# Third stage of a two-block model: projections in f32r on split halves, modulation pieces spread out, their rows turned on VectorE

## The reference

```
x = LN(a*x + even_mixer(x))        # gated delta rule and windowed attention
x = LN(a*x + conv_ffn(x))
x = LN(a*x + odd_mixer(x))         # the third stage: this change
x = LN(a*x + conv_ffn(x))
for i in 0, 1:                     # second block
    shift, scale, gate = split(silu(c) @ ada_w[i, 0] + ada_b[i, 0])   # modulation
    x = LN(a*x + (1 + gate) * mixer(x*(1 + scale) + shift))
    ... the same once more with a mixture of experts in place of the mixer
```

```
q_c, k_c, v_c, q_d, k_d, v_d, r_d, g_d = split(x @ w_in)
lam = exp(sum(lp0*lp1)) - exp(sum(lp2*lp3)) + lam0
o_c = (softmax(q1 k1' + bias) - lam * softmax(q2 k2' + bias)) v_c    # 4 heads, causal
o_c = rms_norm(o_c) * (1 - lam0)
o_d = gated linear attention of (q_d, k_d, v_d) with decay log_sigmoid(g_d @ w + b) / 16
o_d = rms_norm(o_d) * silu(r_d)
out = concat(o_c, o_d) @ w_out
```

## Time and profile before

| | us |
|---|---|
| median of 3 runs | 1826.91 (1821.27 to 1826.99) |
| the profiled execution: span | 1825.7 |
| PE busy | 1750.6 |
| DVE busy | 959.6 |
| ACT busy | 655.1 |
| POOL busy | 229.9 |

### The profile page before, as it was taken

How to read it: one execution, slowest core, us unless ns; L and a number is a source line. 1 busy time by engine, 2 the same in 40 slices (tenths; PEclk the granted TensorE clock), 3 DMA queues, 4 the chain that set the end, 5 groups by cost and what they waited for, 6 DMA issues and landing times. The chain is left out here.

```text
span 1825.7 us, 25869 instructions
## 1 busy us (share of the span) xinstructions
PE 1750.6 (96%) x10464; PEld 1292.0 (71%) x10464; DVE 959.6 (53%) x1782; ACT 655.1 (36%) x1102; POOL 229.9 (13%) x217
## 2 busy tenths in 40 slices
PE   9999999999999999999999989999899999899987
PEld 8788976699887555899888764434489898544433
DVE  1275643688642564788455663333267867533223
ACT  1025323466530234666446431111144455311111
POOL 0000000154211130263002402000000200010000
PEclk9899999999999899999999999999999999999999
DMA  8322286446534585455343659999934555799995
GB/s 309 146 93 92 81 299 267 171 161 223 185 139 162 184 339 214 185 208 185 120 179 139 256 197 421 420 420 419 391 128 160 187 208 207 304 419 420 420 421 228
DMA packets 51853, 443.05 MB, mean 243 GB/s; under 512 B 5900, under 2 KB 6160, under 8 KB 9104
## 3 DMA queue, kind: packets, MB, share of 16 engines
q1 hardware_dynamic: 47664, 426.79, 60.1%
q0 software_dynamic: 2480, 8.92, 1.4%
q10 hardware_dynamic: 1584, 5.61, 0.8%
HBM read 440.25 MB, written 1.05 MB: 242 GB/s over the span
## 5 line engine op out<-in xcount | busy, mean ns | idle before, releaser
L82 PE MATMUL ps<-ringx,arena 128*64 128x512 f32 x1056 | 275.7, 594 | 7.1 <-DMA ringx<-in_mg 3.1
L88 ACT ACTIVATE arena<-ps 128x384 f32<-128x384 f32 (+5 forms) x233 | 101.5, 436 | 495.6 <-PE ps L82 301.4
L82 PE MATMUL ps<-xsplit_f,wsplit_f 128*128 128x256 f32 x2112 | 256.1, 284 | 4.2 <-ACT xsplit_f L88 2.7
L82 PEld LDWEIGHTS ps<-xsplit_f,wsplit_f 128*128 128x128 f32 x2112 | 254.1, 192 | 6.6 <-ACT xsplit_f L88 4.2
L82 PE MATMUL ps<-ring,arena 128*64 128x512 f32 (+1 forms) x704 | 228.0, 597 | 7.5 <-DMA ring<-in_mu 6.1
L91 DVE TENSOR_TENSOR wsplit_f<-ring,wsplit_f 128x1024 fp32r<-128x1024 f32 x132 | 180.5, 1371 | 70.0 <-ACT wsplit_f L88 70.0
L82 PEld LDWEIGHTS ps<-ringx,arena 128*64 128x64 f32 x1056 | 90.2, 137 | 168.3 <-issue 153.9
L82 PE MATMUL ps<-xTs,ring 128*128 128x256 f32 (+1 forms) x960 | 188.8, 357 | 2.3 <-ACT xTs L88 1.8
L82 PEld LDWEIGHTS ps<-xTs,ring 128*128 128x128 f32 x960 | 163.5, 193 | 24.6 <-issue 6.4
L88 ACT ACTIVATE wsplit_f<-ring 128x1024 fp32r<-128x1024 f32 x132 | 138.2, 1051 | 57.5 <-PE ps L82 56.5
L91 DVE TENSOR_TENSOR ringlo<-ring,ringhi 128x1024 fp32r<-128x1024 f32 x88 | 120.7, 1387 | 58.1 <-ACT ringhi L88 57.9
(11 more groups left out here) (196 smaller groups left out, 2452.5 us busy)
## 6 DMA issues: line engine op xcount, KB each, us to landing
ring<-in_ada SPq DMA_DIRECT2D x24, 2048.0 KB, 7.8
ring<-in_wu SPq DMA_DIRECT2D x22, 2048.0 KB, 8.1
ringx<-in_mg SPq DMA_DIRECT2D x44, 1024.0 KB, 20.7
ringx<-in_mu SPq DMA_DIRECT2D x44, 1024.0 KB, 23.9
ringx<-in_md SPq DMA_DIRECT2D x44, 1024.0 KB, 26.1
ring<-in_md SPq DMA_DIRECT2D x24, 1024.0 KB, 25.4
ring<-in_mg SPq DMA_DIRECT2D x24, 1024.0 KB, 20.8
ring<-in_mu SPq DMA_DIRECT2D x24, 1024.0 KB, 23.9
```

Of the source, the lines that this page charges most:

```text
L82: return self.e.matmul(o, l, r, start=start, stop=stop, skip_group_check=True)
L88: return self.e.activation(o, i, f, **k)
```

## The change

- The projections of the stage other than the first four tiles and the small gate product: po4 to po15, "vc", "vd" and the down projection go through `tile_split`, `rows_split`, `rows_half` and `down_split` on split halves. That is 28 parts (`ODD_CH`): 28 high halves on ACT, 28 low halves on DVE, written over the weights in the ring. x is split too (`xth`, `O.xtl`), and the outputs (`O.ohi`, `O.olo`).
- The modulation pieces: four stand ahead of the loop, the others sit at other places in `AMONG`; `LOADS` has them between the other weights, and `BESIDE` and a rule of the oldest slot place them.
- The row block of a piece is turned on DVE: `flip32` transposes its 32x32 blocks into SBUF, in place of ACT's copy, and PE's second product has 32 columns of weights (`fold32`) and 4 columns moving, in four column groups. This holds for the pieces of the first stage as well.
- The causal mask is added to the bias table once at the end of the first stage, in place of in the third.

```
-AMONG = [("po", 12), ("ada", 0), ("po", 13), ("ada", 1), ("po", 14), ("po", 15), ("vd", 0), ("ada", 2), ("vd", 1)] \
-    + [("ada", k) for k in range(3, ADA)]
+AMONG = [("po", 12), ("ada", 4), ("po", 13), ("ada", 5), ("po", 14), ("ada", 6), ("po", 15), ("vd", 0), ("vd", 1),
+         ("ada", 7), ("ada", 8), ("ada", 9), ("ada", 10), ("ada", 11), None, ("ada", 12), None, None]
...
+ODD_CH = chunks("T", ("wo", 1), ("wo", 2)) + chunks("R", ("wov", 0)) + chunks("T", ("wo", 3)) + chunks("R", ("wov", 1)) \
+    + chunks("D", ("woo", 0), ("woo", 1))
...
-    out += [("wo", 0), ("wo", 1), ("wo", 2), ("wov", 0), ("wo", 3)] + ada[:3] + [("wov", 1)] + ada[3:]
+    out += [("wo", 0), ("wo", 1), ada[0], ("wo", 2), ada[1], ("wov", 0)] + ada[2:4] + [("wo", 3)] + ada[4:7] + [("wov", 1)]
+    out += ada[7:] + [("woo", 0), ("woo", 1)] + ffn(1)
...
+BESIDE = {("ada", 3, 0): ("ada", 2, 4), ("wov", 1): ("ada", 2, 5), ("ada", 3, 1): ("ada", 3, 0), ("ada", 3, 2): ("wo", 3),
+          ("ada", 3, 3): ("wov", 1), ("ada", 3, 4): ("ada", 3, 1), ("ada", 3, 5): ("ada", 3, 2), ("woo", 0): ("ada", 3, 3),
+          ("woo", 1): ("ada", 3, 4)}
... (ada_piece on PE)
-                t.wait_ge(*a("adr", i, j))
+                t.wait_ge(*v("adr", i, j))
                 b = bank("ada", i, j)
+                blocks = adr[(k - 1) % 2].rearrange("p (m a n) -> p a n m", m=4, a=4)
                 for c in range(4):
-                    r = mm(b[:, c:c + 1], adr[(k - 1) % 2][:, 128 * c:128 * c + 128], four, True, True)
+                    r = mm(b[32 * c:32 * c + 32, 0:4], fold32, blocks[:, c, 0, :], True, True)
... (odd on PE)
             for n in range(9, 12):
-                proj_T(("wo", 2), "po", n, n % 4, 3)
-            proj_rows(("wov", 0), "vc", 512)
+                tile_split(2, n - 4, "po", n)
+            ada_piece(1, 1)
+            rows_split(2, 8, "vc")
+            ada_piece(1, 2)
+            ada_piece(1, 3)
             for u, k in DIFF:
... (odd on DVE)
+            for i in range(9, 12):
+                low_half(2, i)
+            ada_piece(1, 1)
             for h in range(2):
                 evac_rows("vc", h, O.vc[:, h, :])
-            tt(O.TC, TP, bc(K("cm").rearrange("p (a n) -> p a n", a=1), [128, 4, 256]), ALU.add).then_inc(s_dve, v.did())
+            for i in range(12, 15):
+                low_half(2, i)
+            ada_piece(1, 2)
+            ada_piece(1, 3)
...
+                kind, j = AMONG[k] or (None, 0)
+                if kind == "po":
+                    low_half(2, j + 3)
+                elif kind == "vd" and j == 0:
+                    low_half(2, 19)
+                elif kind == "ada":
                     ada_piece(1, j)
+                if 14 <= k < 18:
+                    low_half(2, k + 6)
```

More of the change, by code:

```diff
@@ L273, in all_slots @@
         else:
-            if name in ELSEWHERE:
-                i = ELSEWHERE[name]
-            else:
-                i = turn % SLOTS
-                turn += 1
+            if name in BESIDE:
+                i = out[BESIDE[name]][0]
+            else:
+                i = min(range(SLOTS), key=lambda k: (LOADS.index(last[k]) if k in last else -1, k))
+            turn = i + 1
         used[i] = used.get(i, 0) + 1
@@ L461, in emit @@
     scb = gate[:, 0:256].rearrange("p (k n) -> p k n", k=8)
-    four = small[:, 218:219]
+    fold32 = gate[:, 256:288]
     fold16 = small[:, 380:396]
@@ L559, in emit @@
         O.oT = rows(O.oTf, 8, 256)
-        O.TC = m.take(1024).rearrange("p (h n) -> p h n", h=4)
+        O.xT = O.oT
         O.gdT = m.take(256)
@@ L572, in emit @@
         O.qd, O.kdT, O.kdt, O.Sg = (rows(m.take(256), 2, 128) for _ in range(4))
+        low_part = m.top
+        m.take(2048)
+        O.rhi = fr(st, "odd_high", 4, 1024)
+    with ExitStack() as st:
+        st.enter_context(nc.sbuf_tensor("below_odd_x", [128, low_part], F32))
+        O.xtl = fr(st, "odd_xlow", 8, 256)
+    with ExitStack() as st:
+        O.ohi, O.olo = (fr(st, f"odd_out{i}", 8, 256) for i in range(2))
     with ExitStack() as st:
@@ L779, in down_part, with x_low, rows_half @@
                 t.note("used", src)
+        def x_low(n):
+            return O.xtl if n == 2 else xtl
+        def rows_half(n, i, tag, h):
+            b, tk = bank(tag, h), slice(h * 128, h * 128 + 128)
+            for c in range(4):
+                _, hi, lo = chunk(n, i + c)
+                t.wait_ge(*v("split", n, i + c))
+                for k in range(2):
+                    for q, (w, xx) in enumerate(((hi, xth), (lo, xth), (hi, x_low(n)))):
+                        r = mm(b, xx[:, 2 * c + k, tk], w[:, k, :], c + k + q == 0, (c, k, q) == (3, 1, 2))
+                if h and c < 3:
+                    r.then_inc(s_pe, t.did())
+                    t.note("part", n, i + c)
+            r.then_inc(s_pe, t.did(tag, h))
+            if h:
+                t.note("part", n, i + 3)
+                t.note("used", CHUNKS[n][i][0])
         def tile_split(n, i, tag, j, ring=R8):
@@ L1219, in odd, with gla_sums @@
                     .then_inc(s_pe, t.did("glo", h))
-            banks = [bank(("dn", 2), i) for i in range(4)]
-            t.wait_ge(*v("dfn", 1))
-            down_part(banks, ("woo", 0), O.oT, (0, 1))
-            for n in range(2):
-                t.wait_ge(*a("gl_sq", n))
-                rms_sums(("gln", n), O.two[n])
-            t.note("early", 2)
-            down_part(banks, ("woo", 0), O.oT, (2, 3))
-            t.wait_ge(*v("gl_out", 1))
-            down([("woo", 0), ("woo", 1)], ("dn", 2), O.oT, banks)
+            def gla_sums():
+                for n in range(2):
+                    t.wait_ge(*a("gl_sq", n))
+                    rms_sums(("gln", n), O.two[n])
+                t.note("early", 2)
+            down_split(2, ("dn", 2), 20, lambda f: O.ohi[:, f, :], lambda f: O.olo[:, f, :], lambda f: v("osplit", f // 2),
+                       {2: gla_sums})
             t.note("pre", 2)
@@ L1715, in ada_piece @@
         def ada_piece(s, k):
+            if 0 <= k < 12:
+                i, j = 2 * s + k // 6, k % 6
+                v.wait_ge(*t("adr", i, j))
+                if k > 1:
+                    v.wait_ge(*t("ada", 2 * s + (k - 2) // 6, (k - 2) % 6))
+                v.own()
+                v.flip32(adr[k % 2], ps("adr", i, j)).then_inc(s_dve, v.did("free", "adr", i, j))
+                v.note("adr", i, j)
             if k <= 0:
@@ L1756, in even @@
                 if n == 6:
-                    red(four, ident[:, 0:128:32], ALU.add).then_inc(s_dve, v.did())
+                    red(fold32, ident.rearrange("p (a j) -> p j a", a=4), ALU.add).then_inc(s_dve, v.did())
                     v.wait_ge(*a("sc"))
@@ L2049, in odd @@
                 stt(o, o, C("lnw"), O.rT[:, n * 512:n * 512 + 512], ALU.mult, ALU.mult).then_inc(s_dve, v.did("gl_out", n))
+            for n in range(2, 4):
+                low_out(n)
+            for i in range(25, 28):
+                low_half(2, i)
             v.note("early", 2)
@@ L2059, in gates @@
             v.note("gdT")
+        def gates():
             v.wait_ge(*t("lga"))
@@ L2763, in odd @@
             stage_begins(1)
-            x_transposed(2, after(1))
+            x_transposed(2, after(1), (xth, O.xtl), xT=O.xT)
+            for i in range(4):
+                high_half(2, i)
             for n in (4, 5, 6, 7):
                 tile(n)
+                high_half(2, n)
+            high_half(2, 8)
             a.wait_ge(*v("la"))
@@ L2773, in odd @@
             a.note("lam")
-            for n in (10, 11):
-                tile(n)
+            high_half(2, 9)
+            tile(10)
+            high_half(2, 10)
+            tile(11)
+            for i in range(11, 15):
+                high_half(2, i)
             Bq = O.Bc.rearrange("p (n t m) -> p n t m", n=2, t=2)
```

116 lines of the change are left out of this document (74 added, 42 removed).

## The result

The changed kernel takes 1844.3 us (1841.8 to 1847.5, 4 runs), the kernel before on the same chip 1827.0 us (1821.3 to 1828.2): ratio 1.0099 with a 95% interval of 1.0083 to 1.0115. That is 17.3 us slower, where 1829.5 us and no measurable change were forecast, and it lies above the range of 1810 to 1841.

A forecast was written before the change was run, and what follows sets the result against it. PE was taken to bound the kernel before, DVE the changed loop. Third stage + 8.6 and first stage - 6.0 gave + 2.6 on the profiled 1825.7; with the runs' median 1.2 above that, 1829.5 us, range 1810 to 1841.

The forecast's parts named there:

- What PE loses in work: Third stage's tiles, row products, down projection and pieces: 28 us less PE work, and 6 in the first stage.
- First stage, - 6: First stage: twelve cheaper second products save 8.0 us, of which 2.0 run into the wait for "woe"; 6 remain.
- First stretch, + 11.2: Third stage up to the loop: PE idles 9.7 us for a turn behind halves of `wo` 3; loop begins 11.2 later.
- The splits of `wo` 1 are ready by then: Third stage's start: with ACT free from 543.5 and DVE from 542.9, splits are ready when f32 tiles end near 550.5.
- the rule that the prediction weighed and priced at 0.15 us: Low halves beside POOL's adds: the skill says POOL contends with DVE's two-input instructions; the rows gave 0.15 us more.
- Loop up to low half 16: Loop's first part: low half 16 waits for the `wov` 1 load; DVE idles 12.3 us, PE about 10.
- Loop from there, 62.9 + 8 us: Loop from low half 16 to "glo": DVE is the bound, with 62.9 us of work and 8 allowed for waits.
- Third stretch: From "glo" to the stage's end: 29.8 us, before 33.5; next stage's second turn 2.5 us later behind the end.
- A: The two waits don't both bind, or DVE's gaps in the loop are shorter: 1818.5 us, chance 0.22.
- C: DVE bounds the loop from 636 to 706, slowed by POOL, with PE clock loss behind pauses: 1841 us, chance 0.20.
- B: PE stays the bound throughout: 1793 us, up to 5 less if the clock stays up, chance 0.08.
- D: Pieces' new second product gains nothing: + 6 in the first stage, hidden in the loop; 1835, within the forecast's 0.50.

The follow-up runs named there:

- e9: e6 with DVE making each of the nine low halves 15 to 23 twice, 18 more instructions: kernel 4.8 us longer than e6.
- e13: The kernel before with only 28 idle PE products added in the third stage's loop: ratio 1.0019.
- e6: The changed kernel with `wo` 3 and `wov` 1 loaded early into other slots, pieces from 3 on made later in the loop: 1827.7 us.
- e8: e6 with 28 idle products on PE ahead of its waits in the third stage's loop: 1822.5 us.
- e1: The kernel before with only the modulation pieces' part of the change (row turned on DVE, new second product): 1820.2 us, ratio 0.9971.
- e12: e7 with the 28 idle PE products in the third stage's loop: 1824.3 us, ratio 0.9984.
- e11: e1 with the 28 idle PE products in the third stage's loop: 1816.4 us, ratio 0.9952.
- e7: e6 with the third stage's last product taken back to f32: 1822.0 us, ratio 0.9977.
- e4: The changed kernel with DVE's turns of pieces 2 and 3 ahead of low halves 12 to 14 and `wov` 1 asked for earlier: 1834.3 us.
- e5: e4 with the third stage's last product taken back to f32, without its low and high halves: 1827.8 us.
- e14: The changed kernel with the 28 idle PE products in the third stage's loop, its late loads left: 1846.6 us, ratio 1.0116.

## Why the prediction was wrong

The sum was 14.7 us short: 8.3 in the loop, 3.2 ahead of it, 2.1 behind it, and the rest in no part that can be named. The step that failed is the loop's sum over DVE alone: 62.9 us of work, which was about right, and 8 us for its waits, which took 17.3.

**What PE loses in work: right.** A tile is 24 products 0.12 us apart, the second product of a piece takes 0.22 to 0.24 (0.25 was taken, between 0.13 and 0.92), the turn 0.72 (0.69). Over all PE's busy time fell by 28.8 us of the 34 counted; some of the work ran at the lower clock. The rows, PE's in the first stage:

```profile
291.16 0.22 PE L82 MATMUL ps<-tmpn,gate 128*32 128x4 f32 x8
292.18 0.24 PE L82 MATMUL ps<-tmpn,gate 128*32 128x4 f32 x8 [0.80 <-DVE tmpn L111]
295.21 4.97 PE L82 MATMUL ps<-ring,arena 128*128 128x512 f32 x7 [2.79 <-DMA ring<-in_woe]
```

**First stage, - 6: right.** "woe" is waited for longer (2.8 us, before 1.4). The profiled executions are 9.9 us apart at the third stage's start, but of this 3.5 is the clock's (last section); two executions alike in that, e9 and e13, start it at 520.98 and 527.36: 6.4 us.

**First stretch, + 11.2: the wait right, the stretch 3.2 short.** PE idled 9.8 us where 9.7 was worked out, behind the instruction named. The stretch grew by 14.4. The 3.2 are two more waits of PE for low halves, 3.8 us where 0.5 was counted. For the first, 2.0 us at 542 and 546, the sentence that failed is "The splits of `wo` 1 are ready by then". It had DVE free from 542.9 on the clock of the execution before, which is 533.0 here; DVE was then at the splits of x and stayed there to 539. DVE, POOL and PE at that place:

```profile
533.52 5.52 DVE L91 TENSOR_TENSOR odd_xlow<-arena,xth 128x512 fp32r<-128x512 f32 x2
538.96 6.69 DVE L91 TENSOR_TENSOR ringall<-ring,odd_high 128x1024 fp32r<-128x1024 f32 x2
```
```profile
533.28 11.29 POOL L91 TENSOR_TENSOR xs<-xs,lnp 128x1024 f32<-128x1024 f32 x4 [7.08 <-ACT arena L88]
```
```profile
542.47 0.36 PE L82 MATMUL ps<-xth,odd_high 128*128 128x256 f32 x1 [1.87 <-DVE ringall L91]
...
579.44 0.50 PE L82 MATMUL ps<-odd_high,xth 128*128 128x512 f32 x1 [1.76 <-DVE ringall L91]
```

The wait of 1.76 us is the second, for low half 9, which the prediction priced at 0.5; no POOL instruction runs there. DVE takes that half only at 578.17, behind the gate's scans.

In the first wait two splits of 0.7 us each took 5.5 and two of 1.22 took 6.7, just while POOL added rows of 128x1024 at 2.8 us each (2.4 each in the kernel before, where no split stood beside them). This is the rule that the prediction weighed and priced at 0.15 us: the Trainium skill (GPSIMD Engine Reference, Specifications) lets POOL contend with VectorE's instructions of two SBUF inputs. The trace agrees, and by 2 us for each instruction, but at a place where the prediction hadn't looked.

**Loop up to low half 16: the waits right, 2.3 us short.** DVE idled 13.7 us there (12.3 worked out), PE 8.7 (about 10); the stretch took 28.5 us in place of 26.2.

**Loop from there, 62.9 + 8 us: wrong, and this is the step that decides.** From the start of low half 16 to the glo products it was 76.9 us in place of 71.0. "So the bound has changed engines", said the prediction; it expected DVE over 85% busy. DVE was busy 59.6 of 76.9 us, 78%, PE 74%. So its row was no longer than worked out, but its idle time, of which 8 us were allowed, was 17.3. Neither is the bound by itself. Units and levels go from PE to DVE, to ACT or POOL, and back; both engines take them in one fixed order, and each stands idle for a part of the other's time. On e6, e9 prices DVE's work at 0.4 to 0.6 of its length, and e8 shows that more work on PE doesn't lengthen the loop. To add up one engine's row and to put a small allowance on it gives a lower bound of such a loop, not its length. The kernel before had PE busy 91.3 and DVE 55.7 of its loop's 98.6 us; with 8.7 less on PE and 8.0 more on DVE the loop took 97.4 (e1), with 16.6 less on PE, 18.5 more on DVE and no late load 98.6 (e6).

The second part of the same step is the clock. The prediction left it to the rivals at 2 us. The tile that follows PE's first pause shows its price, in PE's timeline after:

```profile
603.20 0.58 PE L82 MATMUL ps<-xth,odd_high 128*128 128x256 f32 x1
603.58 0.41 PE L82 MATMUL ps<-odd_xlow,odd_high 128*128 128x256 f32 x1
603.79 0.41 PE L82 MATMUL ps<-xth,ringall 128*128 128x256 f32 x1
...
606.34 0.28 PE L82 MATMUL ps<-xth,odd_high 128*128 128x256 f32 x1
606.46 0.28 PE L82 MATMUL ps<-odd_xlow,odd_high 128*128 128x256 f32 x1
```

Products follow each other in 0.21 us at first and in 0.12 from 606.1: the lower and the higher of the two levels. So the tile takes 4.3 us instead of 2.86. An engine that waits more often also works more slowly. What idle products got back of this in the loop was 1.9, 1.7 and 3.6 us (e8, e12, e11), in e12 lost again in the tail.

**Third stretch: 29.8 us worked out, 32.4 measured; second turn + 2.0 (2.5).** The products themselves are right, but they start in pieces as halves and left sides come. Against the kernel before the tail loses 0.9 us instead of winning 1.2.

**The sum.** Worked out: - 6.0 + 11.2 - 1.4 - 1.2 = + 2.6. Measured by the same parts: - 6.4 + 14.4 + 6.9 + 0.9 = + 15.8; the 17.3 us between the medians leave 1.5, within what the stages behind the fourth differ by from one execution to another (901.0 to 906.2 us).

**By parts of the change**, from differences of stage: the two late loads 15.2 us (after, e6); the split last product 3.6 of loop and tail (e6, e7; 5.9 in e4, e5); twelve tiles and row products on halves 7.3 (e7 against e1), less the 2.9 of e7's clock ahead of the loop, though they spare PE 14; the pieces - 1.2, and in the first stage - 6.4. Of the change only this last part surely pays.

The 7.3 us are not in the loop, which is 1.6 shorter in e7 than in e1. Ahead of it stand 5.8, of which 2.9 are the clock. In the tail stand 3.1, and they are the same instructions behind a wait for POOL at a granted clock of 0.76 (688.2 to 702.5) in place of 1.00, e1 first, then e7:

```profile
686.76 4.30 PE L82 MATMUL ps<-arena 128*128 128x128 f32 x24
690.99 7.13 PE L82 MATMUL ps<-ring,arena 128*128 128x512 f32 x16
```
```profile
688.19 6.08 PE L82 MATMUL ps<-arena 128*128 128x128 f32 x24 [1.60 <-POOL arena L91]
694.21 8.43 PE L82 MATMUL ps<-ring,arena 128*128 128x512 f32 x16
```

**The rivals.** A fell: the waits were both there. C came nearest in size (1841), in part by luck: of its causes the clock held, but DVE was not the bound from 636 to 706, and the mark it gave for itself failed, since the nine low halves in the loop took 1.45 us in the mean, not over 1.8 (one, beside POOL's add, took 2.28). POOL's contention cost PE 2.0 us ahead of the loop; what it cost in the loop wasn't separated. B and D fell.

**Open.** Why the loop stays near 98 us in e6 though PE has 16.6 us less of work is in part argued: DVE's work, the clock and e6's two waits for pieces were not taken apart. That POOL's row sums hold DVE at the stage's start wasn't tested by moving them.

## What to carry to other kernels

Work taken off the fullest engine is worth its length only while that engine has no wait in the stretch; once two engines hand small units to each other, double or pad the work of each in turn, and use the share that comes out instead of a sum over one of them. Before reading a difference, compare the stretches in which both kernels have the same instructions: what they differ by there is noise. A load whose slot comes free by the step ahead of its use costs its whole latency to everyone who stands behind it in each queue: mend it by the order of the loads, since moving one of the waiting instructions only passes the wait on. And where PE has gone from full to three quarters, look at the granted clock; a few idle products ahead of its waits were worth 2 to 4 us of loop here, nothing beside pauses of over 8 us, and cost 1.5 where PE had few waits.

## What the runs showed of the hardware

**The clock can fall without a pause.** In the first stage the kernels differ up to 200 us only by one small sum on DVE at 36 us, yet the windows 60 to 100 do, and after and e9 have no difference at all there. In order: the kernel before, after, e9, each with PE's row full or nearly so.

```profile
60.00:100.00 40.00, 40.00 (x163) 29.39 (x162) 15.94 (x37) 5.64 (x17) 0.00 (x0) 0.87 0.36 135
```
```profile
60.00:100.00 40.00, 40.00 (x182) 29.77 (x181) 15.51 (x37) 6.51 (x19) 0.00 (x0) 0.96 0.37 139
```
```profile
60.00:100.00 40.00, 39.41 (x186) 29.72 (x185) 16.21 (x38) 6.50 (x19) 0.00 (x0) 1.00 0.38 139
```

In the kernel before PE's row shows no idle time when the level falls, in the middle of this stretch:

```profile
75.00:80.00 5.00, 5.00 (x40) 4.79 (x39) 0.00 (x0) 0.38 (x1) 0.00 (x0) 1.00 0.78 256
80.00:85.00 5.00, 5.00 (x17) 3.16 (x17) 1.79 (x10) 1.46 (x7) 0.00 (x0) 0.61 0.69 292
85.00:90.00 5.00, 5.00 (x19) 3.94 (x18) 4.08 (x8) 0.73 (x3) 0.00 (x0) 0.50 0.01 3
```

What PE did before was 32 products of only 12 columns (76.6 to 80.1). e9 and e13 do the same and stay at 1.00. Among kernels with the same instructions up to there the third stage starts between 520.98 (e9) and 527.49 us (e14), and two profiles that differ in this mislead by as much about the start of every later stage. In the same way e7 fell to the lower level from 543.3 to 546.7 and from 580.8 to 584.2 us, and e6 with the same instructions did not. What decides it no run here shows.

**A turn of 128x512 on DVE out of PSUM takes 0.72 us**, as much as a copy (0.69).

**Two-input instructions on DVE can last four times as long beside POOL's adds of 128x1024** (2.76 in place of 0.7 us). In the loop, beside its adds of 128x512, a low half of 1.22 us took 1.46 to 1.49 where it began 0.3 to 0.4 us ahead of an add's end, and 2.28 (at 705.72) where it began 1.2 us ahead of one; adds with such a low half beside them took up to 2.08 us in place of 1.27.
